# The last expert's down projection in two column halves, with its sums shared by ScalarE and VectorE

## The chip, the cores and the metric

The kernel runs on one core of a Trainium2 chip. The metric is device time in microseconds (us) of one execution. The kernel before took 1308.93 us, the median of three runs (1307.45 to 1309.98).

## The reference

One layer of a hybrid encoder: 256 tokens of width 2048. A normed projection feeds three token mixers, an output projection is added to the residual x, and then comes a mixture of experts. All of the change lies in the end of that last part:

```python
hid = jax.nn.silu(xb @ w_gate[e]) * (xb @ w_up[e])      # 2048 -> 512, per expert
y   = hid @ w_down[e]                                   # 512 -> 2048
out = segment_sum(y * gate, token)                      # each token has two experts
x   = x + out
```

There are 32 experts; each has 4 MB (float32) of gate, up and down weights. Each of the 256 tokens goes to two of them, so an expert has about 16 tokens. The kernel gives each expert one item of 32 slots, with further items for an expert that has more tokens.

## The kernel before, in words

The 32 items are worked off in eight quads of four: the first and the last are written out, the middle ones are a loop. SP issues all weight transfers in one queue, one matrix after another into four double buffers ("twins"). For the very last item the up and the down matrix come as two transfers each, into the halves of a twin (`apart`, L314 to L316; the issue is L471). A down half is two of the four 128-row chunks f of the 512 hidden rows, with all 2048 output columns: 16 KB in a row of memory for each partition.

An item goes through these steps (`item_step`, TensorE from L1669):

- Gate and up matmuls, L1699: 16 chunks of 128 rows against 32 slots, spread over four column groups of 32 of the array, so that four partial sums lie in the four partition groups of one bank. ScalarE (L872) and VectorE (L1351) copy them out; `fold_part` (L1679) adds the four groups up and turns them.
- ScalarE's SiLU (L878) and VectorE's product (L1358) give hidT.
- Down matmuls, L1745: for each chunk f and each quarter n of the columns one matmul of 32 slots by 512 columns into partition group n of the bank `b_down`. A half is eight matmuls. For the last item six small matmuls (`keep_clock`, L1409) stand ahead of the second half, and three ahead of the first.
- ScalarE (L889, upper 64 partitions) and VectorE (L1363, lower 64) copy `b_down` into y_item.
- `combine` (L1639 to L1650): for each of the two token tiles t and each quarter n one matmul with 32 rows (gate weights by slot and token, `give`, against y_item) into bank n of `b_comb`. VectorE's `accumulate` (L1333 to L1338) adds each 128x512 result onto the residual in `x_acc`: eight additions per item. The combine of t=1 waits for the addition that frees its bank.

For every item but the last, combine and accumulate are done under the next item's gate and up matmuls. After the last item they stand alone at the end (L1394, L1395, L1769, L1770). SP then stores `x_acc` in eight pieces of 256 KB, each waiting for its addition (L500 to L505), and waits for all of them. Further items would run before the stores; in this profile there are none.

## Time and profile before

| what | value |
|---|---|
| median of three runs | 1308.93 us |
| span of the profiled execution | 1306.6 us |
| TensorE matmul busy | 1066.2 us, 82% |
| VectorE busy | 510.3 us, 39% |
| ScalarE busy | 280.6 us, 21% |
| mean HBM transfer rate | 361 GB/s |
| store of the output | 8 issues of 256 KB |

No time is given for the profiled execution other than its span, 1306.6 us. It is 2.3 us less than the median and lies 0.85 us below the lowest of the three runs. Times inside the profile are us from the start of that span. A matmul in float32 shows as two records, so x16 are eight matmuls.

### The profile page before, as it was taken

The page shows a single profiled execution, that of the slowest core. Times are in us where ns is not written, and L with a number is a line of the kernel's source. Part 1 is how long each engine was busy: PE and PEld are TensorE (multiplying, and loading weights), DVE is VectorE, ACT ScalarE, POOL GpSimd, SP SyncE. Part 2 cuts the span into 40 slices and gives each one's busy share as a digit, 9 for nine tenths or more (in the row PEclk, how much of TensorE's full clock was granted, in tenths as well). Part 3 has the DMA queues.
Part 4 walks back from the last instruction along what each step waited for, and adds up shares of the span by engine and source line. Part 5 has one row for each costly group of instructions (what it writes and reads, how often), then busy time and mean ns, then how long its engine had stood idle before and what let it go on. Part 6 is the DMA issues. An engine that isn't in the chain of part 4 may idle for free.

```text
span 1306.6 us, 17772 instructions
## 1 busy us (share of the span) xinstructions
PE 1066.2 (82%) x7343; PEld 596.3 (46%) x7343; DVE 510.3 (39%) x817; ACT 280.6 (21%) x444; POOL 57.2 (4%) x72
## 2 busy tenths in 40 slices
PE   7999999999999968768677766976786787668667
PEld 7888888888874333224223222422242242224223
DVE  6646677775544453223222222322232242223223
ACT  7445576684430000000000000000000000000000
POOL 3000011501000000000000000000000000000000
PEclk9999999999999988878878888878788797888878
DMA  9965554745678999999999999999999999999996
GB/s 324 292 192 173 158 185 137 249 130 183 276 307 343 427 434 431 428 432 431 431 432 432 433 430 429 433 432 431 431 432 431 432 433 432 429 431 431 431 426 276
DMA packets 83856, 471.61 MB, mean 361 GB/s; under 512 B 7154, under 2 KB 68192, under 8 KB 69216
## 3 DMA queue, kind: packets, MB, share of 16 engines
q1 hardware_dynamic: 83808, 470.94, 88.3%
q8 instruction: 34, 0.56, 0.2%
q14 instruction: 14, 0.11, 0.0%
HBM read 468.83 MB, written 2.10 MB: 360 GB/s over the span
## 4 chain that ended last, share of the span: by engine, by line
DMA 53%; PE 43%; DVE 1%; ACT 1%; issue 1%; POOL 1%; SPq 0%; DVEq 0%; ACTq 0%
DMA twin<-in_w_gate 18%; DMA twin<-in_w_down 18%; PE banks L1467 16%; DMA twin<-in_w_up 15%; PE banks L1469 8%; PE banks L1699 7%; PE banks L1745 4%; PE banks L1649 2%; DMA ring<-in_w_down 2%; PE banks L1665 1%; PE banks L1488 1%; PE banks L1409 1%; PE banks L1679 1%; POOL h_tok L555 1%; PE banks L1520 0%
## 5 line engine op out<-in xcount | busy, mean ns | idle before, releaser
L1699 PE MATMUL banks<-twin,x_exp 128*32 128x512 f32 x1760 | 256.9, 710 | 113.9 <-DMA twin<-in_w_gate 88.9
L1338 DVE TENSOR_TENSOR x_acc<-x_acc,banks 128x512 f32<-128x512 f32 x256 | 158.8, 683 | 350.1 <-PE banks L1649 350.0
L1467 PE MATMUL banks<-hT,w_split 128*128 128x512 f32 x576 | 203.9, 398 | 0.1
L990 DVE TENSOR_TENSOR w_split<-ring,w_split 128x1024 fp32r<-128x1024 f32 x116 | 146.8, 1284 | 113.3 <-ACT w_split L676 112.6
L1745 PE MATMUL banks<-twin,hidT 128*32 128x512 f32 x864 | 144.4, 830 | 46.7 <-DMA twin<-in_w_down 45.8
L1699 PEld LDWEIGHTS banks<-twin,x_exp 128*32 128x32 f32 x1760 | 50.6, 120 | 271.0 <-issue 133.6
L1469 PE MATMUL banks<-hT,w_split 128*128 128x256 f32 x576 | 161.2, 280 | 0.0
L676 ACT ACTIVATE w_split<-ring 128x1024 fp32r<-128x1024 f32 x116 | 121.8, 1060 | 122.8 <-PE banks L1469 122.8
L1467 PEld LDWEIGHTS banks<-hT,w_split 128*128 128x128 f32 x576 | 108.0, 188 | 25.4 <-issue 0.3
L889 ACT ACTIVATE y_item<-banks 64x512 f32<-64x512 f32 x32 | 18.9, 591 | 467.1 <-PE banks L1745 467.1
L1469 PEld LDWEIGHTS banks<-hT,w_split 128*128 128x128 f32 x576 | 108.7, 189 | 0.2
L1363 DVE COPY y_item<-banks 64x512 f32<-64x512 f32 x32 | 22.2, 694 | 210.4 <-PE banks L1745 210.4
L1745 PEld LDWEIGHTS banks<-twin,hidT 128*32 128x32 f32 x864 | 35.9, 145 | 132.8 <-issue 105.7
L872 ACT ACTIVATE gate_sb<-banks 128x512 f32<-128x512 f32 x32 | 19.1, 597 | 341.2 <-PE banks L1699 341.2
L1649 PE MATMUL banks<-y_item,give 32*128 32x512 f32 x512 | 91.0, 757 | 1.7 <-ACT y_item L889 0.9
L1467 PE MATMUL banks<-w_split,y_parts 128*128 128x512 f32 x256 | 91.7, 402 | 0.0
L1469 PE MATMUL banks<-w_split,y_parts 128*128 128x256 f32 x256 | 71.9, 281 | 0.0
L1679 PE MATMUL banks<-fold,up_sb 128*128 128x32 f32 x256 | 34.2, 278 | 42.1 <-DVE up_sb L1351 42.1
L1665 PEld LDWEIGHTS banks<-pick,x_perm 128*128 128x128 f32 x512 | 60.1, 198 | 11.3 <-issue 7.6
L1665 PE MATMUL banks<-pick,x_perm 128*128 128x128 f32 x512 | 61.9, 283 | 3.5 <-DVE x_exp L1328 3.5
L1649 PEld LDWEIGHTS banks<-y_item,give 32*128 32x128 f32 x512 | 26.8, 225 | 80.5 <-issue 77.5
L1679 PEld LDWEIGHTS banks<-fold,up_sb 128*128 128x128 f32 x256 | 31.0, 191 | 70.9 <-DVE x_acc L1338 55.2
(244 smaller groups left out, 864.2 us busy)
## 6 DMA issues: line engine op xcount, KB each, us to landing
twin<-in_w_gate SPq DMA_DIRECT2D x28, 4096.0 KB, 33.2
twin<-in_w_up SPq DMA_DIRECT2D x27, 4096.0 KB, 31.8
twin<-in_w_down SPq DMA_DIRECT2D x27, 4096.0 KB, 33.9
ring<-in_w_in SPq DMA_DIRECT2D x20, 2048.0 KB, 9.4
ring<-in_w_up SPq DMA_DIRECT2D x10, 2048.0 KB, 17.4
ring<-in_w_down SPq DMA_DIRECT2D x10, 2048.0 KB, 18.3
ring<-in_w_out SPq DMA_DIRECT2D x8, 2048.0 KB, 8.3
ring<-in_w_gate SPq DMA_DIRECT2D x7, 2048.0 KB, 14.1
```

Of the source, the lines that this page charges most:

```text
L676: act.activation(w_hi[:, k], src, ACT.Copy).then_inc(hi_ready, 1)
L872: act.activation(gate_sb[:, :].rearrange("p (f k) -> p f k", f=FC), b_gate[:, :].rearrange("p (k f) -> p f k", f=FC), ACT.Copy).then_inc(g ...
L990: dve.tensor_tensor(w_lo[:, k], src, w_hi[:, k].bitcast(F32), ALU.subtract).then_inc(lo_ready, 1)
L1338: dve.tensor_tensor(dst, dst, b_comb[n][:, :], ALU.add).then_inc(acc_done, 1)
L1363: dve.tensor_copy(y_item[k % 2][P // 2:P, :], b_down[P // 2:P, :]).then_inc(y_out_dve, 1)
L1467: pe.matmul(dst[:, 0:2 * PW], stationary[:, 0, cols], moving.rearrange("p s n -> p (s n)"), start=(k == 0 and cc == 0), stop=False)
L1469: ins = pe.matmul(dst[:, PW:2 * PW], stationary[:, 1, cols], moving[:, 0, :], start=False, stop=(k == 3 and cc == 3))
L1649: pe.matmul(b_comb[n][:, :], give[par][rows, t, :], y_item[par][rows, :], start=True, stop=True).then_inc(comb_full, 1)
L1665: ins = pe.matmul(b_gath[b % 2][:, c * P:(c + 1) * P], x2_perm[:, t, 4 * b + c, :], pick[:, t].rearrange("p i s -> p (i s)"), start=(t == ...
L1679: ins = pe.matmul(to[:, f * SLOTS:(f + 1) * SLOTS], part[:, f * P:(f + 1) * P], fold[:, :], start=True, stop=True)
L1699: ins = pe.matmul(dst[SLOTS * j:SLOTS * (j + 1), :], x_exp[:, c, cols], weights[:, cc * F:(cc + 1) * F], start=(c < 4), stop=(c >= KC - 4))
L1745: ins = pe.matmul(b_down[SLOTS * n:SLOTS * (n + 1), :], hidT[:, f, :], weights[:, ff * D + n * DB:ff * D + (n + 1) * DB], start=(f == 0), ...
```

## The change

The down matrix of the last item comes in two halves of its output columns (all 512 hidden rows, 1024 columns; 4 KB in a row of memory, four rows per partition). Its matmuls, copies and sums are done for the first half and then for the second:

- `last_down(h)`: eight matmuls for half h. Partition group 2n+fh of the bank gets the partial sum of quarter n over the chunks of half fh. The second half uses the bank `b_gate`.
- `last_combine(h)`: four matmuls with 64 rows each (both fh groups of quarter n), for t and n in 0, 1.
- Quarters 0, 1 and 2 of each tile are added by VectorE as before (six additions). For quarter 3 TensorE first puts the residual into a bank, by a matmul of the identity against `x_acc`; the combine matmul adds onto it, and ScalarE copies the sum back to `x_acc`.
- The stores are six instead of eight: two of 512 KB, four of 256 KB.
- The rest of the diff fits the waits of further items to the new counts.

```diff
--- before.py
+++ after.py
@@ SP, weights
-                                sp.dma_start(ring[place][:, :].rearrange("p (c n) -> p c n", n=width),
-                                             piece_source((part + 2 * h) if part < 2 else 4 + h, e)).then_inc(
-                                                 piece_in[place], 16)
+                                src = piece_source(part + 2 * h, e) if part < 2 else column_half(e, h)
+                                sp.dma_start(ring[place][:, :].rearrange("p (c n) -> p c n", n=src.shape[2]),
+                                             src).then_inc(piece_in[place], 16)
...
@@ SP, stores
-            for b in range(8):
-                t, n = b // 4, b % 4
-                sp.wait_ge(acc_done, (NE - 1) * 8 + (b + 1))
-                sp.dma_start(out_t[t][:, n * DB:(n + 1) * DB], x_acc[:, t, n * DB:(n + 1) * DB]).then_inc(out_done, 16)
-            sp.wait_ge(out_done, 16 * 8)
+            for t in range(TILES):
+                sp.wait_ge(acc_done, LAST * 8 + 2 * (t + 1))
+                sp.dma_start(out_t[t][:, 0:2 * DB], x_acc[:, t, 0:2 * DB]).then_inc(out_done, 16)
+            for t in range(TILES):
+                sp.wait_ge(acc_last_act, t + 1)
+                sp.dma_start(out_t[t][:, 3 * DB:4 * DB], x_acc[:, t, 3 * DB:4 * DB]).then_inc(out_done, 16)
+                sp.wait_ge(acc_done, LAST * 8 + 4 + (t + 1))
+                sp.dma_start(out_t[t][:, 2 * DB:3 * DB], x_acc[:, t, 2 * DB:3 * DB]).then_inc(out_done, 16)
+            sp.wait_ge(out_done, 16 * 6)
@@ ScalarE
+            def last_outputs():
+                act.wait_ge(piece_used, LAST * PARTS + 5)
+                act.activation(y_item[1][0:P // 2, :], b_down[0:P // 2, :], ACT.Copy).then_inc(y_out_act, 1)
+                act.wait_ge(comb_full, LAST * 8)
+                act.wait_ge(piece_used, LAST * PARTS + 6)
+                act.activation(y_item[0][0:P // 2, :], b_gate[0:P // 2, :], ACT.Copy).then_inc(y_last_act, 1)
+                for t in range(TILES):
+                    act.wait_ge(comb_full, LAST * 8 + 4 + 2 * (t + 1))
+                    act.activation(x_acc[:, t, 3 * DB:4 * DB], b_kept[t][:, :], ACT.Copy).then_inc(acc_last_act, 1)
@@ VectorE
+            def last_outputs():
+                dve.wait_ge(piece_used, LAST * PARTS + 5)
+                dve.tensor_copy(y_item[1][P // 2:P, :], b_down[P // 2:P, :]).then_inc(y_out_dve, 1)
+                for t in range(TILES):
+                    for n in range(2):
+                        dve.wait_ge(comb_full, LAST * 8 + 2 * t + n + 1)
+                        dst = x_acc[:, t, n * DB:(n + 1) * DB]
+                        dve.tensor_tensor(dst, dst, b_comb[2 * t + n][:, :], ALU.add).then_inc(acc_done, 1)
+                dve.wait_ge(piece_used, LAST * PARTS + 6)
+                dve.tensor_copy(y_item[0][P // 2:P, :], b_gate[P // 2:P, :]).then_inc(y_last_dve, 1)
+                for t in range(TILES):
+                    dve.wait_ge(comb_full, LAST * 8 + 4 + 2 * t + 1)
+                    dst = x_acc[:, t, 2 * DB:3 * DB]
+                    dve.tensor_tensor(dst, dst, b_comb[t][:, :], ALU.add).then_inc(acc_done, 1)
...
@@ TensorE
+            def last_down(h):
+                q, k = QUADS - 1, QI - 1
+                weights = half_of(q, k, 2, h).rearrange("p (f n) -> p f n", f=FC)
+                dst = (b_down, b_gate)[h]
+                landed(q, k, 2, h)
+                for ff in range(FC // 2):
+                    for n in range(2):
+                        for fh in range(2):
+                            rows = slice(SLOTS * (2 * n + fh), SLOTS * (2 * n + fh + 1))
+                            f = fh * (FC // 2) + ff
+                            ins = pe.matmul(dst[rows, :], hidT[:, f, :], weights[:, f, n * DB:(n + 1) * DB],
+                                            start=(ff == 0), stop=(ff == FC // 2 - 1))
+                ins.then_inc(piece_used, 1)
+
+            def last_combine(h):
+                for t in range(TILES):
+                    for n in range(2):
+                        rows = slice(2 * SLOTS * n, 2 * SLOTS * (n + 1))
+                        dst = (b_comb[2 * t + n] if h == 0 else b_comb[t] if n == 0 else b_kept[t])
+                        if h == 1 and n == 0:
+                            pe.wait_ge(acc_done, LAST * 8 + t + 1)
+                        pe.matmul(dst[:, :], give[1][rows, t, :], y_item[1 - h][rows, :],
+                                  start=not (h == 1 and n == 1), stop=True).then_inc(comb_full, 1)
+
+            def last_outputs():
+                last_down(0)
+                pe.wait_ge(acc_done, LAST * 8)
+                pe.wait_ge(give_ready, LAST + 1)
+                outputs_written(LAST + 1)
+                last_combine(0)
+                for t in range(TILES):
+                    pe.matmul(b_kept[t][:, :], ident[:, :], x_acc[:, t, 3 * DB:4 * DB], start=True, stop=False)
+                keep_clock(b_up, 4)
+                last_down(1)
+                pe.wait_ge(y_last_act, 1)
+                pe.wait_ge(y_last_dve, 1)
+                last_combine(1)
```

`b_kept` is `[b_fold, b_down]`. On TensorE, ScalarE and VectorE `last_outputs()` follows the last quad; in the item's own step all three leave before the down matmuls and copies, and the six small matmuls between the old halves are gone with them.

## Rows read from the trace of the kernel before

**Rows 1.** The page: span; the DMA line of its 40 slices.

```profile
span 1306.6 us, 17772 instructions
...
DMA  9965554745678999999999999999999999999996
```

**Rows 2.** Chain of waits, 1225 to the end: start, us, what.

```profile
1239.19 33.72 DMA twin<-in_w_gate
1272.91 0.04 issue
1272.96 3.64 PE banks L1699 x16
...
1295.12 0.02 issue
1295.14 0.60 ACT y_item L889
1295.74 0.20 issue
...
1297.09 0.68 DVE x_acc L1338
...
1300.52 1.89 DVE x_acc L1338 x3
```

**Rows 3.** Timeline 1286 to the end: start, us, engine, instruction, count.

```profile
1289.22 0.29 DVE L1358 TENSOR_TENSOR hidT<-silu_sb,banks 128x128 f32<-128x128 f32 x1 [1.27 <-PE banks L1679]
...
1289.76 1.92 PE L1745 MATMUL banks<-ring,hidT 128*32 128x512 f32 x16
...
1291.62 1.60 PE L1409 MATMUL banks<-ident 128*128 128x128 f32 x12
...
1293.15 1.92 PE L1745 MATMUL banks<-ring,hidT 128*32 128x512 f32 x16
...
1295.14 0.69 DVE L1363 COPY y_item<-banks 64x512 f32<-64x512 f32 x1 [5.64 <-PE banks L1745]
...
1295.94 1.14 PE L1649 MATMUL banks<-y_item,give 32*128 32x512 f32 x8 [0.86 <-ACT y_item L889]
1297.07 3.23 DVE L1338 TENSOR_TENSOR x_acc<-x_acc,banks 128x512 f32<-128x512 f32 x5 [1.23 <-PE banks L1649]
1297.78 4.98 SPq L504 DMA_DIRECT2D out<-x_acc  x8
...
1297.90 3.77 PE L1649 MATMUL banks<-y_item,give 32*128 32x512 f32 x8 [0.82 <-DVE x_acc L1338]
```

**Rows 4.** Down halves: issues on SP's queue, and time to landing of both.

```profile
1260.09 0.80 SPq L471 DMA_DIRECT2D ring<-in_w_down  x2
...
DMA to landing us min/median/max: 27.5/29.8/32.0
```

**Rows 5.** Timeline of the item before's combine, between gate and up matmuls.

```profile
1283.71 1.14 PE L1649 MATMUL banks<-y_item,give 32*128 32x512 f32 x8
1284.78 1.92 PE L1699 MATMUL banks<-ring,x_exp 128*32 128x512 f32 x16
...
1285.23 0.13 PEld L1699 LDWEIGHTS banks<-ring,x_exp 128*32 128x32 f32 x4 [0.30 <-issue]
1285.66 0.13 PEld L1699 LDWEIGHTS banks<-ring,x_exp 128*32 128x32 f32 x4 [0.30 <-issue]
```

**Rows 6.** Windows of 1 us: PE, PEld, DVE, ACT, POOL busy, clock, DMA share, GB/s.

```profile
1291.00:1292.00 1.00, 1.00 (x11) 0.39 (x4) 0.00 (x0) 0.00 (x0) 0.00 (x0) 1.00 0.19 82
1292.00:1293.00 1.00, 1.00 (x11) 1.00 (x10) 0.00 (x0) 0.00 (x0) 0.00 (x0) 1.00 0.00 0
...
1297.00:1298.00 1.00, 0.18 (x5) 0.13 (x2) 0.93 (x2) 0.00 (x0) 0.00 (x0) 1.00 0.00 0
1298.00:1299.00 1.00, 1.00 (x3) 0.66 (x4) 1.00 (x3) 0.00 (x0) 0.00 (x0) 0.64 0.36 137
...
1303.00:1304.00 1.00, 0.00 (x0) 0.00 (x0) 0.00 (x0) 0.00 (x0) 0.00 (x0) 0.50 1.01 369
1304.00:1305.00 1.00, 0.00 (x0) 0.00 (x0) 0.00 (x0) 0.00 (x0) 0.00 (x0) 0.50 0.23 82
```

**Rows 7.** A window with 1 KB packets alone, and the span's last weight transfers.

```profile
28.00:30.00 2.00, 2.00 (x14) 1.79 (x12) 0.74 (x1) 1.80 (x4) 0.00 (x0) 1.00 1.10 349
...
1280.00:1285.00 5.00, 4.72 (x56) 2.15 (x52) 0.92 (x3) 1.15 (x3) 0.00 (x0) 1.00 1.02 433
```

**Rows 8.** Groups by line: ScalarE's copy of a 128x512 bank; count, busy, mean ns.

```profile
L872 ACT ACTIVATE gate_sb<-banks 128x512 f32<-128x512 f32 x32 | 19.1, 597 | 341.2 <-PE banks L1699 341.2
```

**Rows 9.** The last store's issue, then landing times of that one and of the first.

```profile
1302.43 0.33 SPq L504 DMA_DIRECT2D out<-x_acc  x1
...
DMA to landing us min/median/max: 3.7/3.7/3.7
...
DMA to landing us min/median/max: 2.3/2.3/2.3
```

More of the change, by code:

```diff
@@ L218, in hymba_layer @@
         b_gath, b_up_fold, b_comb = [bank[4], bank[5]], bank[4], bank[4:8]
+        b_kept = [b_fold, b_down]
         x_in, par_in, router_in = [sem(f"x_in{t}") for t in range(TILES)], sem("par_in"), sem("router_in")
@@ L265, in hymba_layer @@
         comb_full, acc_done = sem("comb_full"), sem("acc_done")
+        y_last_act, y_last_dve, acc_last_act = sem("y_last_act"), sem("y_last_dve"), sem("acc_last_act")
         gath_full, gath_out = sem("gath_full"), sem("gath_out")
@@ L336, in piece_source, with column_half, last_item @@
             return w_down_p[e][:, (i - 4) * (FC // 2):(i - 3) * (FC // 2), :]
+        def column_half(e, h):
+            return w_down_p[e][:, :, h * (D // 2):(h + 1) * (D // 2)]
+        def last_item(q, k):
+            return closing_quad(q) and k == QI - 1
+        LAST = NE - 1
+        ACC_ACT = 2
         def first_quad(q):
@@ L886, in item_step @@
                                ACT.Copy).then_inc(give_ready, 1)
+                if last_item(q, k):
+                    return
                 act.wait_ge(piece_used, i * PARTS + 6)
                 act.activation(y_item[k % 2][0:P // 2, :], b_down[0:P // 2, :], ACT.Copy).then_inc(y_out_act, 1)
+            def last_outputs():
[7 more added lines that the diff above has]
+                    act.activation(x_acc[:, t, 3 * DB:4 * DB], b_kept[t][:, :], ACT.Copy).then_inc(acc_last_act, 1)
             def quad(q, n_extra=None):
@@ L903, in _ @@
             quad(QUADS - 1)
+            last_outputs()
             act.wait_ge(table_ready, 1)
@@ L1360, in item_step @@
                                   ALU.mult).then_inc(hid_ready, 1)
+                if last_item(q, k):
+                    return
                 dve.wait_ge(piece_used, i * PARTS + 6)
@@ L1393, in _ @@
             quad(QUADS - 1)
-            accumulate(NE - 1, 0)
-            accumulate(NE - 1, 1)
+            last_outputs()
             n_extra = dve.value_load(tab[0:1, 0:1], min_val=0, max_val=NX - 1)
             with dve.If(n_extra > 0):
+                dve.wait_ge(acc_last_act, TILES)
                 with dve.Fori(QUADS, QUADS + XQ) as q:
@@ L1637, in landed, with combine @@
                     pe.wait_ge(piece_in[half_place(q, k, part, h)], half_landed(q, k, part, h))
-            def combine(i, t, par):
+            def combine(i, t, par, further_quad=False):
                 outputs_written(i + 1)
                 pe.wait_ge(give_ready, i + 1)
+                by_act = ACC_ACT if further_quad else 0
                 for n in range(4):
                     if t == 1:
-                        pe.wait_ge(acc_done, i * 8 + n + 1)
+                        pe.wait_ge(acc_done, i * 8 + n + 1 - by_act)
                     elif not (isinstance(i, int) and i == 0):
-                        pe.wait_ge(acc_done, i * 8 + n - 3)
+                        pe.wait_ge(acc_done, i * 8 + n - 3 - by_act)
                     rows = slice(SLOTS * n, SLOTS * (n + 1))
@@ L1657, in gather @@
                 if not first_quad(q):
-                    pe.wait_ge(acc_done, (q * QI - (0 if further_quad else 1)) * 8)
+                    pe.wait_ge(acc_done, q * QI * 8 - (ACC_ACT if further_quad else 8))
                 for b in blocks:
@@ L1725, in item_step @@
                 elif further_quad:
-                    pe.wait_ge(acc_done, i * 8)
+                    pe.wait_ge(acc_done, i * 8 - ACC_ACT)
                 if k == 0:
@@ L1736, in item_step @@
                     outputs_written(i)
+                if ends:
+                    return
                 for h in range(2):
                     weights = half_of(q, k, 2, h)
-                    if ends and h == 1:
-                        keep_clock(b_up, 6)
                     landed(q, k, 2, h)
@@ L1749, in item_step @@
                 if further_quad:
-                    combine(i, 0, k % 2)
-                    combine(i, 1, k % 2)
+                    combine(i, 0, k % 2, True)
+                    combine(i, 1, k % 2, True)
+            def last_down(h):
[33 more added lines that the diff above has]
+                last_combine(1)
             def quad(q, n_extra=None):
@@ L1768, in _ @@
             quad(QUADS - 1)
-            combine(NE - 1, 0, 1)
-            combine(NE - 1, 1, 1)
+            last_outputs()
             pe.wait_ge(table_ready, 1)
@@ L1773, in _ @@
             with pe.If(n_extra > 0):
+                pe.wait_ge(acc_last_act, TILES)
                 with pe.Fori(QUADS, QUADS + XQ) as q:
```

## The prediction

> **What bounds the kernel now.** I first read the slices of the page: over the last two thirds the DMA line stands at 9 and only the very last slice falls [rows 1]. The chain of waits then shows why: up to 1272.91 us the chain is the gate matrix of the last item landing, a transfer; behind it everything is one short chain of engines [rows 2]. So the experts are bound by their 4 MB matrices, which the change leaves as they are up to the last item's down matrix. What can move is the stretch after the last product hidT (1289.22 + 0.29 = 1289.51) up to the end, 17 us out of 1306.6. I read it in the timeline [rows 3]:
>
> - first down half 1289.76 to 1291.68, six small matmuls, second down half 1293.15 to 1295.07;
> - both copies of the bank, the slower being VectorE's, 0.69; TensorE starts combining at 1295.94, which is 0.87 after the last down matmul;
> - the first sum is ready at 1297.07 (1.13 later); then eight additions on VectorE: five for 3.23 us and three from 1300.52, ending 1302.41 [rows 2, 3]. VectorE is the bound of this piece: 5.34 us of additions, against a second combine that only waits for its banks;
> - the last store is issued at 1302.43 and lands 3.7 later, at 1306.13 [rows 9].
>
> Is the second half waiting for data? The down transfers are issued at 1260.09 and about 0.4 later (0.80 for both), and land after 27.5 and 32.0 us: at 1287.6 and 1292.5 [rows 4]. The windows agree: from 1292 on nothing is moved [rows 6]. TensorE starts on them at 1289.76 and 1293.15. Both halves are there before TensorE asks, the second by 0.6 us. That is the key reading: in the kernel before the path behind the landing is already an engine path, and anything put on TensorE ahead of the second half delays it one for one.
>
> **The change part by part.** All times are those of the profiled execution (span 1306.6); the median of runs is 2.3 above it, and I add the difference that I find to the median.
>
> *Transfer in column halves.* The packets shrink from 16 KB to 4 KB rows. The nearest rows are 433 GB/s with large rows and 349 with 1 KB rows [rows 7]; 4 KB lies between. At the worst the 4.2 MB of both halves take 12.0 us in place of 9.7, so the first lands up to 1.2 later (1288.8, before 1289.76) and the second up to 2.3 later (1294.8). Cost zero if the second half is asked for after that, which the next step shows; at best it gains nothing, since no one waits for it. The number of issues is the same.
>
> *First half.* Same eight matmuls over four column groups: 1289.76 to 1291.68 as now.
>
> *Copies and first combine.* The same two copies, so TensorE starts at 1291.68 + 0.87 = 1292.55. The combine is now four matmuls of 64 rows, not four of 32. Four 32-row ones stand side by side in the array: from 1283.71 to the next line's start at 1284.78, 1.07 us in all [rows 5]. Of 64-row ones two fit. The pace of one round of 512 columns is read off the weight loads that are 0.43 apart per record of a round, two records a matmul: 0.86 [rows 5]. So two rounds: 1.07 + 0.86 = 1.93. No row shows a 64-row matmul; the bounds are 1.07 (like the four of 32) and 1.07 + 3 x 0.86 = 3.65 (each alone). I take 1.93, since the rows that they occupy are disjoint in pairs just as in the row read. End 1294.48.
>
> The Trainium skill states the same number of rounds (TensorEngine Tiling (Array Packing), section Tiling Modes: the array makes four tiles of 32 rows, or two of 64, that run independently), and it speaks against the change: the work is the same bytes, yet half as many matmuls go at once, so each combine costs a round more. In "Key Properties" there it also says that a change of tiling mode drains the array. The trace has the price of such a change in the 1.07 above, which is 0.21 over one round; the change has three more of them, and by the rule alone some 0.4 us would be added that I haven't put in for the identity matmuls.
>
> *Four additions of the first half.* VectorE starts at 1292.55 + 1.13 = 1293.68; the second pair comes 0.86 later, so the four run nearly without a gap, 4 x 0.68, to 1296.4 [rows 2, 3]. Hidden: TensorE isn't done with the second half before 1299. These are the additions that the change takes off the tail. Were the cover gone, the second copy would be held by them.
>
> *Residual into the bank.* Two matmuls of the identity with 512 columns over the whole array, nothing beside them: 2 x 0.86 = 1.72. Bounds: 0.43 each if one record did it, and 1.07 each with a start of its own. They read `x_acc` after the item before's additions, long done. They sit on TensorE ahead of the second half: on the path. To 1296.20.
>
> *keep_clock.* Four small matmuls in place of six: 12 records took 1293.15 - 1291.62 = 1.53 [rows 3], so eight take 1.02. To 1297.22.
>
> *Second half.* It starts at 1297.22 and not at 1293.15: 4.07 later. Its data lie there since 1294.8 at the latest. It ends at 1299.14. Copies, 0.87: 1300.01. First pair of sums 1.13 later, 1301.14; second pair 1302.00.
>
> *The new tail.* Per tile one addition on VectorE (0.68) beside one copy on ScalarE (0.60 by the copy of an equal bank [rows 8]). Tile 0 is done at 1301.8, tile 1 at 1302.68. Before: 1302.41. So the tail behind the last down matmul shrinks from 7.34 (1295.07 to 1302.41) to 3.54, a gain of 3.80, and the second half is 4.07 later: net +0.27.
>
> *Stores.* SP now issues tile 1's two stores right behind each other. ScalarE's is first, at 1302.6; the second cannot be issued before that issue is through, 0.40 by the pair of [rows 4]: 1303.0 against 1302.43, 0.57 later. In the old order the stores kept the write stream full: from 1298.64 (0.36 of that window) past 1304, at about 380 GB/s [rows 6], and the last landed 3.7 after its issue where the first took 2.3 [rows 9]. In the new order two of 512 KB are gone early (ready at 1295.1 and 1296.4), and four of 256 KB come from 1301.74 on. Data start 0.86 after an issue (1297.78 to 1298.64): 1302.6; 1.05 MB at 380 GB/s is 2.76, to 1305.4; the first store of before had 2.3 - 0.86 - 0.69 = 0.75 from last data to landing. That gives 1306.15. By the last issue alone it is 1303.0 + 2.3 = 1305.3 at best and 1303.0 + 3.7 = 1306.7 at worst. I take 1306.4 against 1306.13: +0.3.
>
> **Sum.** Second half +4.07, tail -3.80, last issue +0.30 for its place behind ScalarE's store, shorter queue -0.27: +0.3. 1308.93 + 0.3 = 1309.2. The change takes about 4 us of VectorE's work off the tail and puts about 4 us of TensorE's work ahead of the second half.
>
> **Rivals.**
>
> *The 64-row matmuls don't run in pairs.* Slower. Then each combine takes 3.65 in place of 1.93, and both are on the path: the first delays the second half, the second the last sum. +3.4, so 1312.6. For it: no row shows a 64-row matmul, and each record has a weight load ahead of it, which could hold the next pair. Against it: the four of 32 rows, with the same 128 columns, run side by side. It decides as soon as four such matmuls hold TensorE for over 2.5 us.
>
> *TensorE falls to half clock in the second half or its combine.* In the kernel before the granted clock falls from 1.00 to 0.64 and 0.50 (2.4 to 1.2 GHz) in 1298 to 1299, behind a stretch with 0.87 and 0.82 us of idle round a short combine [rows 3, 6]. There it is cheap, since VectorE is the bound. In the changed kernel a second combine at half clock is on the path: two rounds at twice 0.86 are 1.7 more, with its start 2.0: 1311.2. If it reached the down half (1.92 at full clock; 16 records took 3.64 after the wait for the gate matrix [rows 2]), 1.7 more: 1312.9. Against it: from 1292.55 to 1299.14 TensorE is never idle.
>
> *The pieces are cheaper than the rounds say.* Faster. If 64-row matmuls hid their second round behind the load and the copies (1.07 per combine, -0.86 each), and the last store met an empty queue (1305.3 instead of 1306.4, -1.1), the sum would be 0.3 - 2.8 = -2.5: 1306.4. For it: the old stores were queued, the new ones hardly. Against: one round for 64 rows has nothing in the rows.
>
> *The column halves arrive late.* Only if 4 KB rows went below 349 GB/s by much; for the second half at 1297.2 it would need 4.7 us more than now. I give it next to nothing, and it would read 1310 or more.
>
> **How the numbers follow.** Forecast 0.74; pairs don't overlap 0.08; half clock 0.08; cheaper 0.08; late halves 0.02. A change of 0.2% (2.6 us) is about what can be told from none here: 1306.3 to 1311.5. The forecast lies well inside, but the runs of before alone span 2.5 us, so I leave 0.05 of it to either side. Slower: 0.08 from the pairs, half of the clock's 0.08, 0.01 of the late halves and 0.05, in all 0.18. Faster: half of the cheaper case, 0.04, and 0.05, in all 0.09. Same: 0.73. The range reaches from the runs' spread below the forecast to the case of a slower combine: 1307.0 to 1311.8.
>
> **What would show it.** Right: the second down half starts near 1297.2, with DMA idle for 2 us or more before it; combines hold TensorE for about 1.9; VectorE's first four additions end before the second half does; the last addition ends within 0.5 of 1302.7; the last store lands 2.5 to 3.5 after its issue. Wrong: a second half that starts before 1296 (filling cheaper) or waits for its DMA; a combine over 2.5; a clock below 1.00 before 1302; a store that trails past 1307.

## The result

The changed kernel took 1310.62 us (median of 21 runs, 1309.03 to 1313.28) against 1308.61 (21 runs, 1306.91 to 1310.2). The ratio is 1.0017, 95% interval 1.0011 to 1.0023: slower by 2.0 us by the medians and 2.2 by the ratio, clear of noise and inside the 0.2% that the forecast called no change. The forecast was +0.3 us. The time lay in the range; the size of the rise was missed, and most of what follows is about the missing 1.5 to 2 us.

Some differences in spans come from ahead of the change: in the profile of after, the last gate matrix lands at 1274.25 where it was 1272.91 [rows 2]. So I count every trace from the start of its first down half, F: 1289.76 before, 1291.36 after. From F to the end of the span is 16.80 us before and 18.61 after, +1.81, which agrees with the runs.

The profile of before looked fast next to the three runs, because its span was put beside device times. For the changed kernel and for every later run both numbers are on record: the device time lies above the core's span, by 1.7 to 2.3 us in all runs but those of one kernel (TensorE held, below). So the profile of before is an ordinary execution; its span, 1306.6, is also the median span of the later runs of that kernel.

The timeline of the changed kernel from the first down half on (start, us, engine, instruction; answering [rows 3]):

```profile
1291.36 1.92 PE L1812 MATMUL banks<-ring,hidT 128*32 128x512 f32 x16
...
1294.19 1.99 PE L1824 MATMUL banks<-y_item,give 64*128 64x512 f32 x8 [0.91 <-DVE y_item L1402]
...
1295.32 2.48 DVE L1407 TENSOR_TENSOR x_acc<-x_acc,banks 128x512 f32<-128x512 f32 x4 [1.28 <-PE banks L1824]
...
1296.11 1.98 PE L1836 MATMUL banks<-x_acc,ident 128*128 128x512 f32 x4
1296.64 1.53 SPq L514 DMA_DIRECT2D out<-x_acc  x2
...
1297.93 1.05 PE L1456 MATMUL banks<-ident 128*128 128x128 f32 x8
...
1298.91 1.92 PE L1812 MATMUL banks<-ring,hidT 128*32 128x512 f32 x16
...
1301.70 1.99 PE L1824 MATMUL banks<-y_item,give 64*128 64x512 f32 x8 [0.86 <-ACT y_item L914]
...
1303.50 0.33 SPq L517 DMA_DIRECT2D out<-x_acc  x1
1303.69 0.69 DVE L1413 TENSOR_TENSOR x_acc<-x_acc,banks 128x512 f32<-128x512 f32 x1 [0.17 <-PE banks L1824]
1303.73 0.60 ACT L917 ACTIVATE x_acc<-banks 128x512 f32<-128x512 f32 x1 [0.26 <-PE banks L1824]
1303.87 1.07 SPq L519 DMA_DIRECT2D out<-x_acc  x1
1304.99 0.43 SPq L517 DMA_DIRECT2D out<-x_acc  x1
1305.47 0.45 SPq L519 DMA_DIRECT2D out<-x_acc  x1
```

Two things are to be seen. The second half starts 7.55 us after the first (1298.91 - 1291.36) where it was 3.39 [rows 3]: 4.16 later, all of it TensorE's own queue. And SP, which in the kernel before issued its last store 0.02 after the last sum, issues it 1.09 after it (1305.47 against 1304.38), with one issue of 1.07 us in the middle. The windows show TensorE's clock at full and the transfer over before the second half (engines, then clock, DMA share, GB/s; answering [rows 6]):

```profile
1293.00:1294.00 1.00, 0.28 (x4) 0.00 (x0) 0.65 (x1) 0.59 (x1) 0.00 (x0) 1.00 0.20 82
...
1297.00:1298.00 1.00, 1.00 (x4) 0.45 (x3) 0.81 (x2) 0.00 (x0) 0.00 (x0) 1.00 0.53 217
...
1305.00:1306.00 1.00, 0.00 (x0) 0.00 (x0) 0.00 (x0) 0.00 (x0) 0.00 (x0) 1.00 0.61 225
1306.00:1307.00 1.00, 0.00 (x0) 0.00 (x0) 0.00 (x0) 0.00 (x0) 0.00 (x0) 0.98 1.05 381
1307.00:1308.00 1.00, 0.00 (x0) 0.00 (x0) 0.00 (x0) 0.00 (x0) 0.00 (x0) 0.50 0.55 199
1308.00:1309.00 1.00, 0.00 (x0) 0.00 (x0) 0.00 (x0) 0.00 (x0) 0.00 (x0) 0.50 0.09 25
```

The data of the down halves end at 1293.7; from 1297 on it is stores that move. At 1305, with all sums done, the write stream is only 0.61 full: I read that as the stream waiting for issues, not the issues for it. At 1308 a share of 0.09 is left: by my estimate from it one or two of the 16 DMA engines carry the last data, up to 1309.1.

### The profile page after: what moved, and what is told of

Same layout as the page of the kernel before. It is cut to its first block, busy times and chain, and to the rows that moved or that the text cites. A ratio compares the mean times of both kernels' runs of the same rounds, so it can differ in the third digit from the quotient of the medians.

```text
span 1310.0 us, 17772 instructions
## 1 busy us (share of the span) xinstructions
PE 1069.8 (82%) x7343; PEld 598.3 (46%) x7343; DVE 510.0 (39%) x816; ACT 282.3 (22%) x447; POOL 55.9 (4%) x72
## 4 chain that ended last, share of the span: by engine, by line
DMA 53%; PE 43%; DVE 1%; ACT 1%; issue 1%; SPq 0%; DVEq 0%; ACTq 0%
DMA twin<-in_w_gate 18%; DMA twin<-in_w_down 18%; PE banks L1514 16%; DMA twin<-in_w_up 15%; PE banks L1516 8%; PE banks L1747 7%; PE banks L1793 4%; DMA ring<-in_w_down 2%; PE banks L1697 2%; PE banks L1713 1%; PE banks L1535 1%; PE banks L1456 1%; PE banks L1727 1%; DMA x_acc<-in_x 1%; PE banks L1567 0%
## 5 line engine op out<-in xcount | busy, mean ns | idle before, releaser
L1367 DVE TENSOR_TENSOR x_acc<-x_acc,banks 128x512 f32<-128x512 f32 x248 | 153.7, 683 | 347.0 <-PE banks L1697 346.9
L1793 PE MATMUL banks<-twin,hidT 128*32 128x512 f32 x864 | 147.1, 843 | 46.2 <-DMA twin<-in_w_down 45.8
L1697 PE MATMUL banks<-y_item,give 32*128 32x512 f32 x496 | 85.7, 751 | 0.0
```

The lines of the kernel that those rows point to most:

```text
L1367: dve.tensor_tensor(dst, dst, b_comb[n][:, :], ALU.add).then_inc(acc_done, 1)
L1697: pe.matmul(b_comb[n][:, :], give[par][rows, t, :], y_item[par][rows, :], start=True, stop=True).then_inc(comb_full, 1)
L1793: ins = pe.matmul(b_down[SLOTS * n:SLOTS * (n + 1), :], hidT[:, f, :], weights[:, ff * D + n * DB:ff * D + (n + 1) * DB], start=(f == 0), ...
```

## The experiments

All twelve in one table: the ratio to the kernel before with its interval, and four lengths from the profile in us: F to the last sum, last sum to the start of SP's last store issue, that to the end of the span, and their total.

| kernel | ratio (95%) | F to last sum | to last issue | to end | total |
|---|---|---|---|---|---|
| before | 1 | 12.65 | 0.02 | 4.13 | 16.80 |
| after | 1.0017 (1.0011 to 1.0023) | 13.02 | 1.09 | 4.50 | 18.61 |
| no filler | 1.0012 (1.0003 to 1.0021) | 12.14 | 1.44 | 4.63 | 18.21 |
| merged stores | 1.0003 (0.9994 to 1.0012) | 13.03 | 0.07 | 4.67 | 17.77 |
| all on VectorE | 0.9999 (0.9990 to 1.0008) | 12.24 | 0.25 | 4.50 | 16.99 |
| gaps | 1.0000 (0.9991 to 1.0009) | 10.44 | 2.14 | 4.53 | 17.11 |
| padded SP | 1.0016 (1.0007 to 1.0025) | 13.03 | 1.34 | 3.25 | 17.62 |
| gaps + merged stores | 0.9988 (0.9979 to 0.9997) | 10.45 | 0.07 | 4.77 | 15.29 |
| sharing in row halves | 1.0013 (1.0004 to 1.0022) | 11.40 | 1.77 | 4.67 | 17.84 |
| ScalarE's own stores | 1.0014 (1.0005 to 1.0023) | 13.03 | 0.02 | 4.85 | 17.90 |
| TensorE held | 1.0037 (1.0025 to 1.0049) | 13.03 | 0.46 | 5.25 | 18.74 |
| gaps, merged, held | 0.9993 (0.9984 to 1.0002) | 10.44 | 0.07 | 5.75 | 16.26 |
| before, no filler | 1.0002 (0.9993 to 1.0011) | 11.92 | 0.03 | 4.10 | 16.05 |
| before, four stores | 1.0005 (0.9996 to 1.0014) | 12.67 | 0.02 | 4.62 | 17.31 |

The first length is the computation and the change's whole subject. The others are the stores.

There is one trace for each kernel. The differences of the totals and those of the runs agree to 0.7 us in ten of the thirteen rows below the first; they are 1.0 and 1.3 us apart for "before, no filler" and "padded SP", and 2.9 for "TensorE held". So a few tenths of a us in the last three columns tell of one execution, not of the kernel.

### What stands ahead of the second half

No filler:

```diff
-                keep_clock(b_up, 4)
                 last_down(1)
```

> The changed kernel without the four small filler matmuls ahead of the second down half. In its trace TensorE runs without a gap from the first combine to the end of the second half and the data lie there 5 us early. Theory P (the second half is late by TensorE's own queue): the second half starts 1.0 us earlier and the end follows, so +1.0 us against the kernel before in place of +2.0. Rival W (the write stream of the stores sets the end): the first 1 MB of stores is gone long before, so also about -1.0; no difference here. Rival C (the filler holds the clock up): the granted clock falls before the second combine and 1 to 2 us are lost again, +2 or more.

The last sum came 0.88 earlier (12.14 for 13.02; theory P had 1.0), and the clock held at 1.00 (rival C is out). But the whole moved by 0.4 in the trace, and the ratio fell only from 1.0017 to 1.0012, with overlapping intervals: the stores gave half of it back. Their issues:

```profile
1301.12 0.33 SPq L517 DMA_DIRECT2D out<-x_acc  x1
1301.49 1.42 SPq L519 DMA_DIRECT2D out<-x_acc  x1
1302.96 0.43 SPq L517 DMA_DIRECT2D out<-x_acc  x1
1303.44 0.95 SPq L519 DMA_DIRECT2D out<-x_acc  x1
```

Rival W forecast no other time than theory P, so this run says nothing on it.

All on VectorE (the sharing undone, the column halves kept):

```diff
-                for t in range(TILES):
-                    pe.matmul(b_kept[t][:, :], ident[:, :], x_acc[:, t, 3 * DB:4 * DB], start=True, stop=False)
...
-                    dve.tensor_tensor(dst, dst, b_comb[t][:, :], ALU.add).then_inc(acc_done, 1)
+                    dve.tensor_tensor(dst, dst, (b_comb, b_kept)[n][t][:, :], ALU.add).then_inc(acc_done, 1)
```

> The changed kernel with the column halves kept but the sharing undone: no residual matmuls, VectorE adds all four results of the second half, ScalarE none. Theory P: TensorE is 1.98 us earlier at the second half, the tail gets 4 additions behind the first pair in place of one behind the second (1.13 + 4 x 0.68 = 3.87 against 3.54 - 0.87 = 2.67), so 0.8 us faster than the changed kernel, +1.2 against the kernel before; the stores are issued 0.68 apart again. With theory S on top (stores no longer bunched) another 0.5 to 1.0 less, about +0.4. Rival (the sharing is what brings the gain and the residual matmuls are hidden): 1.2 us slower than the changed kernel, +3.2.

The last sum is 0.78 earlier, 0.8 by theory P: the residual matmuls (1.98) cost more ahead of the second half than ScalarE's help brings behind it. With the stores 0.5 to 0.9 apart again, the whole is 1.6 shorter, and the kernel is level with the one before. So the second part of the change, by itself, is a loss where it was put.

Gaps (the residual matmuls moved into the stretches in which TensorE waits for copies):

```diff
                 last_down(0)
...
+                keep_residual(0)
                 outputs_written(LAST + 1)
                 last_combine(0)
-                for t in range(TILES):
-                    pe.matmul(b_kept[t][:, :], ident[:, :], x_acc[:, t, 3 * DB:4 * DB], start=True, stop=False)
-                keep_clock(b_up, 4)
                 last_down(1)
+                keep_residual(1)
...
```

`keep_residual(t)` is the matmul of the identity for tile t that is taken out of the loop.

> The changed kernel with its two residual matmuls moved into the two stretches in which TensorE waits for the copies (0.91 and 0.86 us idle in the trace), and no filler. Theory P: the second half starts 1.98 + 1.05 = 3.0 us earlier, at its data's landing or later, and the end moves with it: 2.6 to 3.0 us faster than the changed kernel, about -0.8 against the kernel before. Rival W (the write stream of all stores sets the end): the first half's stores then still run when the second's begin, and the gain stops at about 2. Rival C (clock falls without the filler): 1 to 2 us of it are lost.

```profile
1291.09 1.12 PE L1830 MATMUL banks<-x_acc,ident 128*128 128x512 f32 x2
...
1292.15 1.99 PE L1824 MATMUL banks<-y_item,give 64*128 64x512 f32 x8
...
1294.06 1.92 PE L1812 MATMUL banks<-ring,hidT 128*32 128x512 f32 x16
...
1299.17 1.86 SPq L519 DMA_DIRECT2D out<-x_acc  x1
1301.08 0.69 SPq L517 DMA_DIRECT2D out<-x_acc  x1
```

A residual matmul in the wait delays the combine behind it by 0.1 (2.91 from a half's start to its combine, for 2.83 and 2.79), and the last sum is 2.58 earlier than in the changed kernel, 2.2 earlier than in the kernel before. Nothing of the 2.2 reaches the end: ratio 1.0000 (theory P had -0.8 us, which the interval doesn't exclude). One store issue now takes 1.86 and the last starts 2.14 after the last sum. The clock stayed at 1.00, so rival C is out here too. Rival W's "about 2" is near the 2.2 us that the ratios give against the changed kernel, but not for its reason: the first half's stores have moved their data by 1298.5, ahead of the second half's first issue at 1298.80, and the time goes in the issues.

### The stores

Merged stores:

```diff
             for t in range(TILES):
                 sp.wait_ge(acc_last_act, t + 1)
-                sp.dma_start(out_t[t][:, 3 * DB:4 * DB], x_acc[:, t, 3 * DB:4 * DB]).then_inc(out_done, 16)
                 sp.wait_ge(acc_done, LAST * 8 + 4 + (t + 1))
-                sp.dma_start(out_t[t][:, 2 * DB:3 * DB], x_acc[:, t, 2 * DB:3 * DB]).then_inc(out_done, 16)
+                sp.dma_start(out_t[t][:, 2 * DB:4 * DB], x_acc[:, t, 2 * DB:4 * DB]).then_inc(out_done, 16)
...
```

> The changed kernel with the second half's stores as one of 512 KB per token tile, so two issues in place of four. Theory S (issuing stores behind each other on SP costs the missing time: in the trace of the changed kernel the four issues start at 1303.50, 1303.87, 1304.99 and 1305.47, the last 1.1 us after the last sum): the last issue starts right behind the last sum, 1.0 to 1.1 us earlier, and the kernel is 0.8 to 1.2 us faster than the changed one, about +1.0 against the kernel before. Rival W (write stream, 1.05 MB at 380 GB/s behind the first of these stores): 0 to -0.4, so about +1.8. Rival L (a late DMA engine after the last issue, 3.7 us wait of SP): no gain, +2.0.

The computation is the same to 0.01 us (13.03), the last issue starts 0.07 behind the last sum, and the ratio is 1.0003: by the two ratios 1.8 us faster than the changed kernel (0.8 in the one trace). A long issue is still there, 1.00 us from 1301.35 on, but it is the last and no other stands behind it. The merged stores also have rows of 4 KB in place of 2 KB; from 401 GB/s over a full window against 381, that is an estimated 0.1 us for their 1.05 MB, so it isn't the cause. The same merging in the kernel before:

```diff
-            for b in range(8):
...
-                sp.wait_ge(acc_done, (NE - 1) * 8 + (b + 1))
...
+            for b in range(4):
...
+                sp.wait_ge(acc_done, (NE - 1) * 8 + 2 * (b + 1))
...
```

> The kernel before with four stores of 512 KB in place of eight of 256 KB: how much of the best version's gain is the stores alone. The first store waits one addition more (0.68 us later), the last covers two additions. In the kernel before the stream of 2.1 MB is full from 1298.64 on at 380 GB/s; with 4 KB rows a window of the changed kernel shows 401 to 410. Theory W (the stream sets the end there): start 0.68 later, 5.2 us long in place of 5.5: +0.3. Theory L (the late engine after the last issue decides): last issue at the same time with twice the data, +0.3 to +0.7.

It isn't a gain there (1.0005; 0.5 longer in the trace): with one sum every 0.68 us on one engine the issues were never bunched. Theories W and L forecast nearly the same, and the interval holds both. Merging repairs something that the change brought in.

Gaps + merged stores, both edits above together:

> Both repairs at once: residual matmuls in the two waiting stretches, no filler, and one 512 KB store per tile for the second half. From the traces: first down half to last sum 10.4 us (as with the moved matmuls) and last sum to the end 4.7 us (as with the merged stores), 15.1 in place of 16.8 in the kernel before: -1.7 us, ratio 0.9987. Rival W (the write stream sets the end): the first half's stores run from about 1295.5 to 1298.2 and the second's begin at 1299, so nothing is queued; if it were, the gain would stop at -0.5.

```profile
1293.69 1.92 PE L1811 MATMUL banks<-ring,hidT 128*32 128x512 f32 x16
1294.25 1.53 SPq L514 DMA_DIRECT2D out<-x_acc  x2
...
1298.55 1.81 SPq L518 DMA_DIRECT2D out<-x_acc  x2
```

0.9988 (0.9979 to 0.9997), 1306.82 against 1308.37: 1.6 us faster than the kernel before and the only one of all that beats it beyond its interval, though by less than the 0.2% that the forecast called no change. -1.7 was expected from adding two columns of the table. The idea of the change brings a little, then, once the order on TensorE and the four stores are mended.

Sharing in row halves (the other half of the change alone):

```diff
...
+                        for t in range(TILES):
+                            pe.matmul(b_kept[t][:, :], ident[:, :], x_acc[:, t, 3 * DB:4 * DB], start=True, stop=False)
-                        keep_clock(b_up, 6)
...
+                for t in range(TILES):
+                    act.wait_ge(comb_full, LAST * 8 + 4 * (t + 1))
+                    act.activation(x_acc[:, t, 3 * DB:4 * DB], b_kept[t][:, :], ACT.Copy).then_inc(acc_last_act, 1)
...
```

> Half of the change alone: the down matrix in halves of its rows as in the kernel before, one y_item, 32-row combines; but the residual of the last quarter is put into banks by TensorE (two matmuls in place of the six fillers between the halves), ScalarE copies these sums back, VectorE adds six. All eight results have banks of their own. Theory P: the second half starts 0.4 later (1.98 for 1.60), the tail loses two of VectorE's eight additions (-1.2 to -1.4): the last sum is 0.9 us earlier. Rival W: the eight stores' stream, full from 1298.6 to 1304.1 in the kernel before, isn't shorter, so the whole gains 0.2 at most: -0.2 us. Without W it would be -0.9.

```profile
1297.63 3.67 DVE L1402 TENSOR_TENSOR x_acc<-x_acc,banks 128x512 f32<-128x512 f32 x6 [1.28 <-PE banks L1813]
...
1298.35 2.06 SPq L515 DMA_DIRECT2D out<-x_acc  x3
...
1300.45 0.46 SPq L517 DMA_DIRECT2D out<-x_acc  x1
1300.95 2.07 SPq L515 DMA_DIRECT2D out<-x_acc  x3
1303.07 0.68 SPq L517 DMA_DIRECT2D out<-x_acc  x1
```

The sums are done 1.25 us earlier than before, at 1301.30, and the kernel is 1.7 us slower. SP issues its eight stores without a pause from 1298.35 to 1303.75 and starts the last of them 1.8 us after the last sum. I had expected the write stream to hold the gain down; what grew was the time of the issues.

### Why an issue takes long

The first theory was SP's own code: a 16 KB packet of the instruction queue shows beside the first long issue of each kernel.

Padded SP:

```diff
+            for _ in range(32):
+                sp.wait_ge(consts_ready, 1)
             for t in range(TILES):
                 sp.wait_ge(acc_done, LAST * 8 + 2 * (t + 1))
```

> The changed kernel with 32 waits on SP, all on a semaphore long reached, put ahead of its first output store. In the traces so far a 16 KB packet of the instruction queue starts 0.1 us after the first store of the second half (changed kernel: 1303.62, lasting 0.96) and SP's next issue ends 0.36 us behind it, in four of five kernels to the hundredth; in the kernel before it starts at 1302.48, after the last issue. Theory F (SP stands for its own code, and where that fetch falls decides): with the longer code the fetch falls into the 30 us in which SP waits, the four issues run without the long one, and the kernel is 0.6 to 1.2 us faster than the changed one, +1.0 to +1.4 against the kernel before. Rival B (an issue close behind another takes long in itself): no change, +2.0, the second issue again at 1 us.

No change in the time (1.0016), and the packet moved only behind the second issue; now the third is long (1.33):

```profile
1300.61 0.33 SPq L519 DMA_DIRECT2D out<-x_acc  x1
...
1300.99 0.43 SPq L521 DMA_DIRECT2D out<-x_acc  x1
1301.47 1.33 SPq L519 DMA_DIRECT2D out<-x_acc  x1
1302.84 0.43 SPq L521 DMA_DIRECT2D out<-x_acc  x1
```

The second issue, close behind the first, takes 0.43, against rival B, which had the time right and its sign wrong. Theory F's forecast failed; by itself that is weak, since 32 waits may be too few to move a fetch, and the traced execution was the fastest of the eleven (1308.36 for a median of 1310.57). The next two kernels say more.

ScalarE's own stores:

```diff
+                for t in range(TILES):
+                    act.wait_ge(acc_last_act, t + 1)
+                    act.dma_start(out_t[t][:, 3 * DB:4 * DB], x_acc[:, t, 3 * DB:4 * DB]).then_inc(out_done, 16)
...
```

SP's two waits and stores for these quarters are taken out.

> The changed kernel with ScalarE's two quarters stored from ScalarE's own queue, so SP has two stores of the second half and not four. Theory S/F (the time goes in SP's issues, one of them behind the fetch): ScalarE's stores no longer stand behind it, but VectorE's second store still does if the fetch falls there: 0.5 to 1.0 us faster than the changed kernel, +1.0 to +1.5. Rival L (a late DMA engine): no gain.

0.7 faster than the changed kernel in the trace and 1.0014 against 1.0017 in the runs, too little to tell. SP's last issue starts on time and takes 0.90. ScalarE's last one starts at 1302.73, 0.04 before it, and takes 0.93: two engines, each with its own code, finish their issues at the same moment, 1303.66 and 1303.67. So what holds an issue is hardly SP's own code.

What moves with the packet is TensorE's end. The traces hold one more record: after its last matmul TensorE loads the number of further items and branches over their code, and that branch instruction takes 3.3 to 4.2 us in all fourteen traces, where VectorE's takes 0.06. The instruction packet starts 1.02 to 1.85 us after the branch does:

| kernel | TensorE's branch starts | packet | its length | store issue beside it |
|---|---|---|---|---|
| before | 1300.87 | 1302.48 | 0.96 | 1302.43, 0.33 us |
| after | 1302.60 | 1303.62 | 0.96 | 1303.87, 1.07 us |
| no filler | 1300.22 | 1301.25 | 1.30 | 1301.49, 1.42 us |
| merged stores | 1299.50 | 1300.53 | 1.21 | 1301.35, 1.00 us |
| all on VectorE | 1300.35 | 1301.38 | 1.04 | 1301.90, 0.89 us |
| gaps | 1298.26 | 1299.29 | 1.37 | 1299.17, 1.86 us |
| padded SP | 1299.75 | 1301.27 | 0.96 | 1301.47, 1.33 us |
| gaps + merged stores | 1297.92 | 1298.94 | 1.05 | 1299.38, 0.98 us |
| sharing in row halves | 1297.48 | 1298.51 | 1.04 | 1298.94, 0.98 us |
| ScalarE's own stores | 1301.00 | 1302.04 | 0.98 | 1302.77, 0.90 us |
| TensorE held | 1304.19 | 1306.04 | 0.96 | none |
| gaps, merged, held | 1300.98 | 1302.35 | 1.20 | none |
| before, no filler | 1301.16 | 1302.74 | 0.97 | 1302.73, 0.33 us |
| before, four stores | 1300.08 | 1301.38 | 1.31 | 1301.76, 0.33 us |

Where an issue just ahead runs into the packet's start as well, the table names the one behind it. The packet alone isn't enough: three issues beside it took 0.33, one of them wholly inside it (1301.76 against 1301.38 to 1302.70). In the traces an issue beside this packet was long when the packet began within 0.49 us of the start of the issue ahead on the same queue, and took 0.33 to 0.43 when it began 0.65 or more behind that start. Three further long issues stand beside other instruction packets and don't all follow this: the 0.95 in the kernel without filler and the 0.69 in gaps beside one of 8 KB, and one of 1.00 in row halves beside the next one of 16 KB.

The Trainium skill has a mechanism for this (Runtime: NRT & Kernel Launch, section Instruction fetch mechanics): code comes in 16 KB blocks by DMA, and a taken branch to a block that isn't there must wait for it. The traces agree on the 16 KB packet and on a long branch, of whose 3.34 us in the changed kernel the packet fills 0.96; what fills the rest isn't shown. That such a packet also holds another engine's store issue is what the next kernel was made to test.

TensorE held behind the last sums:

```diff
             last_outputs()
+            pe.wait_ge(acc_done, LAST * 8 + 6)
+            pe.wait_ge(acc_last_act, TILES)
             pe.wait_ge(table_ready, 1)
```

> The changed kernel, with TensorE held behind the last two sums (waits on VectorE's and ScalarE's last additions) before it loads the number of further items and branches over their code. In ten traces TensorE's branch is followed by a 16 KB packet of the instruction queue, 1.02 to 1.04 us after its start in eight and 1.5 to 1.6 in two, and the store issue of SP that runs while this packet does ends 0.36 to 0.65 behind it. Theory F' (TensorE's code fetch holds SP's issue): the branch moves from 1302.6 to about 1304.8, the packet to 1305.8, the four issues of the second half take 0.33 to 0.45 each and the last starts 0.6 us earlier: the kernel is 0.4 to 0.8 us faster than the changed one, +1.2 to +1.6 against the kernel before. Rival B (an issue close behind another is long by itself): the long issue stays, +2.0. Rival L (the packet only delays one DMA engine's share of the data, wherever it falls): the long issue goes and the time stays, +2.0.

```profile
1302.11 0.33 SPq L517 DMA_DIRECT2D out<-x_acc  x1
...
1302.49 0.43 SPq L519 DMA_DIRECT2D out<-x_acc  x1
1302.97 0.45 SPq L517 DMA_DIRECT2D out<-x_acc  x1
1303.46 0.45 SPq L519 DMA_DIRECT2D out<-x_acc  x1
```

The branch moved to 1304.19, the packet to 1306.04, and the long issue is gone: four issues as close as ever, 0.33 to 0.45. Rival B falls. The last starts 0.46 behind the last sum, not 1.09, so of the 1.07 us that the change lost here (1.09 - 0.02), 0.63 hang on TensorE's branch and 0.44 on four issues in a row. The data gain more than that: the last store lands 4.10 behind the last sum, where it was 5.19 in the changed kernel and 3.76 in the kernel before. From the last moment with eight or more DMA packets under way to the end of the data it is 0.9 us and not 1.6. So rival L, with the landing as late as ever, isn't borne out in the trace either.

The time didn't follow: 1.0037 (six runs), slower, which no theory had. SP's waits at the end show part of the cause (waiter, releaser: us, times, longest):

```profile
SPq L93 <- DMA out<-x_acc: 3.2, 1, 3.2
SPq L93 <- PEq L93: 1.4, 1, 1.4
```

After the last store has landed the kernel waits 1.4 us more for TensorE, whose branch ends at 1308.35, 0.36 before the span does. In the other kernels, the next one apart, that second wait is 0.2. Of the 4.5 us by which the median is above the kernel before, 2.0 lie in the spans (medians 1308.6 and 1306.6). The other 2.5 lie outside the core's span: in the six runs the device time is 3.8 to 4.4 above the span. What the chip does there no profile shows.

Gaps, merged, held:

> The best version so far (residual matmuls in the two waiting stretches, no filler, one 512 KB store per tile) with TensorE held as well. Theory F': the last store's issue takes 0.4 in place of 0.98 us and no DMA engine is taken while the stores are set up, -0.3 to -0.6 us beside the version without the hold, so -1.9 to -2.2 against the kernel before (0.9984). Rival L: the packet then falls on an engine amid the last data, no gain, -1.6.

```profile
SPq L93 <- DMA out<-x_acc: 3.2, 1, 3.2
SPq L93 <- PEq L93: 2.0, 1, 2.0
```

The same price inside the span: 2.0 us of waiting for TensorE. (Outside of it there is none, the device time is 1.7 to 1.9 above the span.) The last store lands 3.64 behind the last sum, where it was 4.44. The issue of the last store takes 0.33 and was 0.98, and the kernel isn't faster for it (0.9993 against 0.9988, not told apart; 1.0 longer in the trace). Its expectation missed because I had not added up the branch's 3.9 us behind the new start.

Before, no filler:

```diff
-                    if ends and h == 1:
-                        keep_clock(b_up, 6)
```

> The kernel before without the six small matmuls between the down halves. It tests the reading that its second half was not waiting for data: the second down transfer lands at 1292.5, TensorE asks at 1293.15. Theory P: the second half starts 0.6 us earlier, now at its landing, and the time falls by 0.4 to 0.6 us (0.9996). Rival (the fillers hide a wait for data in most runs): no change, 0.0. Rival C (they hold the clock up): the second half or the combines at half clock, +0.5 to +2.

```profile
1290.78 1.92 PE L1743 MATMUL banks<-ring,hidT 128*32 128x512 f32 x16
...
1293.45 1.92 PE L1743 MATMUL banks<-ring,hidT 128*32 128x512 f32 x16 [0.75 <-DMA ring<-in_w_down]
```

The second half now starts 2.67 behind the first, for 3.39 [rows 3], and does wait for its data: the slack was 0.7 in this execution, 0.6 by my reading. The last sum is 0.73 earlier in the trace; the runs show no gain (1.0002). So the order behind the landing was an engine's, by little, as read. Of the times, the interval (0.9993 to 1.0011) holds both the forecast 0.9996 and no change. Rival C is out: the clock falls in 1298 to 1300, 8.6 us behind F, and in the kernel before it was 8.5.

## Why the prediction was right in kind and short in size

*The computation.* Nearly as worked out. The second half 4.16 later (4.07 forecast): combine 1.92 up to the next start (1.93), residual matmuls 1.82 (1.72), fillers 0.98 (1.02). The 64-row matmuls run in pairs; that rival is out. The tail from the last down matmul to the last sum is 3.55 (3.54). Net +0.37 at the last sum against +0.27. The kernel without the filler and the one without the sharing each moved the last sum by what the sum of terms says, to 0.1 us (0.88 for 1.0, 0.78 for 0.8).

*The column halves' transfer.* Hidden, as said. Its data end at 1293.7, 5 us before they are asked for.

*The clock.* It stayed at 1.00 until the last matmul, in the changed kernel (until 1306.96) and in every variant of it; the rival had no case here.

*The last issue.* This is the step that failed: "the second cannot be issued before that issue is through, 0.40 by the pair of [rows 4]: 1303.0 against 1302.43, 0.57 later". From the last sum to the last issue I had 0.32; it was 1.09. I let only the last store wait for its neighbour, and took no issue to be longer than 0.40. In fact the four stand in one row at 0.43 to 0.45 (0.44 of it, by the held kernel), and TensorE's branch fetches code amid them (0.63).

*The drain.* Forecast to be 0.3 shorter than before, since the queue is empty; it is 0.37 longer (4.50 for 4.13). The stream was not full any more, because the issues fed it too slowly: 0.61 busy at 1305. The held kernel, with the packet behind nearly all of the data, says what most of it hangs on: from its last issue to the landing it is 3.63, where the changed kernel has 4.10 and the kernel before 3.73. So of the 1.43 us by which the last landing behind the last sum grew (5.19 for 3.76), 1.09 went with TensorE's branch moved, and 0.34 stayed with four stores issued in a row. The prediction had this length at 3.72 (1306.4 less 1302.68).

Together: +0.37, +1.07 and +0.37 are the +1.81 of the trace. The forecast had +0.27, +0.30 and -0.27. That the time lay in the range all the same is luck in part: the range reached up to 1311.8 for a slow combine, which didn't come, and not for the stores. Of the prediction's own signs those of the computation came true (less the 1.60 by which F is later, the second half starts at 1297.31 and the last addition ends at 1302.78), and those of the stores failed: the last landing is 4.10 behind its issue, not 2.5 to 3.5, and it trails past 1307 (1307.97 less the same 1.60).

*What I should have seen.* The page has an instruction queue with 34 packets in section 3, and the chain of waits ends in the stores; I worked out bytes per us for them, took only one of SP's issues into the sum, and left the instruction queue out.

Shown by runs: that merging the stores takes back 1.8 us of the changed kernel's time, and that order and stores mended together beat the kernel before. Shown by traces, one for each kernel: what the order on TensorE costs up to the last sum, and that the long issue goes and the landing comes earlier when TensorE's branch is moved (in two pairs of kernels). Not shown: how a code packet holds an issue or a landing, and what 2.5 of the 4.5 us are that holding TensorE cost in the runs. A kernel in which the branch's target is loaded early was not tried.

## What to carry to other kernels

Work that is put ahead of a step to shorten what follows it is paid in full unless it stands in a wait; moving the same two matmuls out of the line into the two stretches in which TensorE waited for copies brought the last sum forward by 1.7 us (12.14 without filler, 10.44 in gaps), and the time by 1.6 (ratios 1.0012 and 1.0000). When a tail is made parallel, count the issues of its stores as a serial chain of their own: results that come in pairs want one store. And a kernel's last microseconds belong to whatever each engine does last, a branch over unused code among it: it is not in the busy time, and it can be both in the way (early) and the end (late).

## What the runs showed of the hardware that was not expected

- A branch of TensorE over the unused code of the further items takes 3.3 to 4.2 us (fourteen traces); VectorE's over its own takes 0.06.
- A store issue beside a 16 KB instruction packet took 0.89 to 1.86 us in nine traces, on SP's queue and on ScalarE's, where it takes 0.33 alone and 0.43 to 0.45 close behind another. It took 0.33 beside the packet in three traces, where the packet began 0.65 us or more behind the start of the issue ahead.
- With TensorE's branch moved behind the last sums, the last store landed 1.09 and 0.80 us earlier behind the last sum (two pairs of kernels).
- The device time lies 1.7 to 2.3 us above the core's span, and 3.8 to 4.4 in the kernel with TensorE held.
- Matmuls of 64 rows by 128 columns run two at a time: four of 512 columns, each two records, in 1.99 us; four of 32 rows in 1.14 [rows 5]; two of 128 rows in 1.98.
- Stores in 4 KB rows show 401 to 410 GB/s over full windows of 1 us and those in 2 KB rows 379 to 383.
